# Sums of squares of the six pre-norms: TensorE reads the eight tiles of squares itself, VectorE adds nothing

## The reference

```
def _rmsnorm(x, w):
    xf = x.astype(jnp.float32)
    y = xf * lax.rsqrt(jnp.mean(xf * xf, -1, keepdims=True) + NORM_EPS) * w
    return y.astype(x.dtype)
...
    for i in range(DEPTH):
        hh = _rmsnorm(x, norm_w[i, 0])
        x = x + FFN_RES * _rmsnorm(_swiglu(hh, ...), norm_w[i, 1])
        hh = _rmsnorm(x, norm_w[i, 2])
        m = _even_mixer(hh, ...) if i % 2 == 0 else _odd_mixer(hh, ...)
        x = x + _rmsnorm(m, norm_w[i, 3])
        hh = _rmsnorm(x, norm_w[i, 4])
        x = x + FFN_RES * _rmsnorm(_swiglu(hh, ...), norm_w[i, 5])
```

## Time and profile before

| | |
|---|---|
| three runs | 3228.89, 3232.3, 3232.4 us; median 3232.3 |
| the profiled execution's own time | 3232.59 us |
| its span (first to last instruction) | 3230.8 us |
| mean granted TensorE clock | 0.933 |
| TensorE busy | 2871.7 us, 89% |
| DVE busy | 1560.4 us, 48% |
| ACT busy | 1034.4 us, 32% |
| DMA read | 240.79 MB, 75 GB/s |

### The profile page before, as it was taken

One profiled execution on the slowest core, in us unless ns is written; L12 is line 12 of the kernel. 1 busy time (PEld: TensorE's weight loads), 2 busy tenths in 40 slices (PEclk: granted clock), 3 DMA queues, 4 the chain that ended last, 5 costly groups with the idle time before them and its releaser, 6 DMA issues. The chain is left out here.

```text
span 3230.8 us, 37354 instructions
## 1 busy us (share of the span) xinstructions
PE 2871.7 (89%) x15512; PEld 2261.2 (70%) x15512; DVE 1560.4 (48%) x2191; ACT 1034.4 (32%) x1538; POOL 6.8 (0%) x10
## 2 busy tenths in 40 slices
PE   5999999999999997336779999999998769899998
PEld 1476677577888786226758888788886559778886
DVE  1157446635434533673256434553446476464244
ACT  0135334533223313330134223332233532342222
POOL 0000000000000000000000000000000000000000
PEclk9899979999999998667889999999998989999998
DMA  8121202112232332000012232233322110022322
GB/s 365 78 79 59 78 30 82 66 53 79 85 111 79 96 99 72 0 0 1 1 46 85 85 110 78 89 101 93 104 85 79 59 46 4 28 85 85 107 86 69
DMA packets 65112, 245.30 MB, mean 76 GB/s; under 512 B 7216, under 2 KB 7344, under 8 KB 63536
## 3 DMA queue, kind: packets, MB, share of 16 engines
q1 hardware_dynamic: 64656, 238.72, 22.8%
q0 software_dynamic: 288, 4.19, 0.4%
HBM read 240.79 MB, written 2.10 MB: 75 GB/s over the span
## 5 line engine op out<-in xcount | busy, mean ns | idle before, releaser
L346 PE MATMUL bank<-normed,weights_high 128*128 128x512 f32 x4848 | 1530.4, 397 | 45.8 <-ACT normed L1172 42.1
L346 PEld LDWEIGHTS bank<-normed,weights_high 128*128 128x128 f32 x4848 | 913.4, 190 | 272.9 <-issue 81.8
L346 PE MATMUL bank<-normed,weights_low 128*128 128x512 f32 x2424 | 953.1, 393 | 0.0
L1665 DVE TENSOR_TENSOR weights_low<-ring,weights_high 128x1024 fp32r<-128x1024 f32 (+2 forms) x431 | 484.5, 1127 | 516.8 <-ACT weights_high L1206 513.3
L1206 ACT ACTIVATE weights_high<-ring 128x1024 fp32r<-128x1024 f32 (+2 forms) x431 | 420.7, 979 | 934.6 <-PE bank L346 934.4
L346 PEld LDWEIGHTS bank<-normed,weights_low 128*128 128x128 f32 x2424 | 460.6, 190 | 96.9
L346 PE MATMUL bank<-hidden,weights_high 128*128 128x512 f32 x1408 | 433.3, 389 | 0.0
L346 PE MATMUL bank<-work 128*128 128x128 f32 (+7 forms) x1912 | 262.9, 354 | 74.5 <-DVE work L1936 50.2
L346 PEld LDWEIGHTS bank<-hidden,weights_high 128*128 128x128 f32 x1408 | 264.3, 188 | 54.8
L1880 DVE TENSOR_TENSOR silu_gate<-bank,rstd 128x512 f32<-128x512 f32 x176 | 120.9, 691 | 341.0 <-PE bank L346 336.1
L346 PE MATMUL bank<-hidden,weights_low 128*128 128x512 f32 x704 | 273.9, 389 | 0.0
(11 more groups left out here) (205 smaller groups left out, 1942.0 us busy)
## 6 DMA issues: line engine op xcount, KB each, us to landing
ring<-w_k SPq DMA_DIRECT2D x303, 512.0 KB, 3.5
work<-w_ada SPq DMA_DIRECT2D x6, 4096.0 KB, 20.9
ring<-w_d SPq DMA_DIRECT2D x64, 384.0 KB, 3.0
ring<-w_d SPq DMA_DIRECT2D x64, 320.0 KB, 2.9
work<-dft_in POOLq DMA_DIRECT2D x2, 2048.0 KB, 8.4
constants<-cst_in SPq DMA_DIRECT2D x1, 2656.0 KB, 8.9
residual<-x_in SPq DMA_DIRECT2D x1, 2048.0 KB, 13.6
out_dram<-residual SPq DMA_DIRECT2D x8, 256.0 KB, 2.1
```

Of the source, the lines that this page charges most:

```text
L346: return pe.matmul(o, lhsT, rhs, start=start, stop=stop, skip_group_check=True)
L1665: ve.tensor_tensor(WL[:, u % SPLIT, 0:w], RING[:, u % SLOTS, 0:w], WH[:, u % SPLIT, 0:w].bitcast(F32), ALU.subtract).then_inc(unit_split, 1)
```

## The change

`pre_rms` takes the place of the one-part call at all three places that a pre-norm's `rms_of` is called from: TensorE now reads all eight tiles of squares, waiting for ACT's `sq` of each, and adds them in bank 7. `sum_of_squares` is gone from VectorE's program.

```diff
@@ project, ffn, odd_projection (TensorE)
-                        rms_of(("pre", name), (tile(0), dve_done("sum", name)))
+                        pre_rms(name)
@@ TensorE
+            def pre_rms(name):
+
+                rms_of(("pre", name), *[(tile(k), act_done("sq", name, k)) for k in range(KT)])
@@ VectorE
-            def sum_of_squares(name):
-
-                for n in (4, 2, 1):
-                    for k in range(n):
-                        dve.wait_ge(*act_done("sq", name, k + n))
-                        if n < 4:
-                            dve.wait_ge(*dve_done("sums", name, 2 * n + k + n))
-                        d(ve.tensor_tensor(tile(k), tile(k), tile(k + n), ALU.add),
-                          *(("sum", name) if n == 1 else ("sums", name, n + k)), chain=False)
-
             def pre_norm(name, w, lows_first):
 
-                sum_of_squares(name)
                 for j in range(LEAD):
                     low(lows_first + j + SPLIT)
```

More of the change, by code:

```diff
@@ L658, in ffn @@
                         if q == 0 and j == LEAD:
-                            rms_of(("pre", f), (tile(0), dve_done("sum", f)))
+                            pre_rms(f)
                     u0, n = UNIT0[f"down{f}{q}"], half // 2
```

## The result

The changed kernel took 3305.7 us in the median of four runs (3301.8 to 3309.3), the kernel before 3232.35 in the median of its four beside it: a ratio of 1.0205, interval 1.0177 to 1.0233. The forecast was 3302. A second measurement, further down, gives 1.0204. Two single runs are left out of every ratio here, one of the kernel before at 4000.8 us and one of `two_tiles_mix0` at 3528.0, with mean granted clocks of 0.70 and 0.80.

A forecast was written before the change was run, and what follows sets the result against it. TensorE's stream was taken to set the time at the norms. Five norms at 12.5 us plus mix1 at 10.2 made 72.7 on 3232.3, or 3305.0, lowered to 3302; the 8-in-10 range was 3276 to 3317.

The forecast's parts named there:

- What bounds the kernel: At five norms TensorE's stream alone sets the time; behind mix1 it waits for chains of DVE and ACT.
- the two covers named for the additions: VectorE's 28.8 us of additions hide behind TensorE's first four units and DVE's 2.55 us idle before the reciprocal: 0 us.
- The passes: At each pre-norm, 56 added one-column passes at 0.112 us each cost 6.3 us at full clock.
- The clock: Falls to 0.50 about 2.9 us into each norm's passes: 3.9 us more on passes, 2.3 on work behind.
- the rival in which it holds: Clock stays 1.00 at the norms, so only the passes count: 37.6 us, 3270; chance 0.07 for all or most norms.
- the slow part behind: Low clock lasts 3.0 to 6.9 us behind each norm's passes and costs 1.4 to 3.2 us, taken as 2.3.
- Mix1: At this norm 6.3 + 3.9 lie before `ms`; TensorE's waits take up the 2.3 behind, so 10.2 us.
- The sum: Whole kernel: 5 x 12.5 + 10.2 = 72.7 us on 3232.3, giving 3305.0, lowered to 3302.
- Mixers hiding the delay: Rival: chains behind mix0 and mix1 have room for all their delay, leaving 50 us, 3282; chance 0.05.
- Nearly free passes: Rival: the 56 passes a norm take 0.025 us each, 8.4 us in all, without a clock fall: 3241; chance 0.02.
- Faster: Rival: additions were late for unit 4, so removing them saves at most 4.5 us a norm: 3213 at best; chance 0.01.

The follow-up runs named there:

- two_tiles_mix0: Kernel before, but at pre-norm mix0 alone VectorE does six of seven additions and TensorE reads two tiles, 8 passes more: ratio 0.9997.
- no_additions: Changed kernel, but TensorE reads tile 0 alone as before the change, and VectorE's 42 additions stay removed: 3236.5 us, ratio 0.9995.
- in_between: Changed kernel, but each tile's eight one-column passes stand behind that tile's three matmuls in the unit before: 3284.6 us, ratio 1.0143.
- half-width run: Changed kernel, but of tiles 1 to 7 only 64 of each 128 tokens are loaded as weights: 3277.7 us, ratio 1.0111.
- passes_alone: Kernel before with VectorE's 42 additions kept, but TensorE reads eight tiles behind the last addition: 3299.5 us, ratio 1.0191.

## Why the prediction was right, and where it was off

*What bounds the kernel* was read rightly. TensorE's stream sets the time at the norms, and `no_additions` gives back nothing, by its ratio and by its steps. Of the two covers named for the additions, TensorE's units were there. The idle 2.55 us before the reciprocal wasn't the second one: it stays as it was in `no_additions`, and what covered them on DVE is its wait for ACT's high part of unit 4.

*The passes.* 0.112 us at full clock and 6.3 us a norm: `in_between` shows 6.35 at five norms. The half-width run shows that the load makes the price.

*The clock.* It fell at all six, as in the layer norms, and the rival in which it holds fell with that. The size was off for the reason the prediction gave as open: behind dense products it holds longer, 3.9 to 5.0 us at five norms in place of 2.9. At pre-norm 10 the passes took 9.22 us where 26 at 0.112 and 38 at 0.214 make 11.0. So this term was 3.9 a norm and measured about 2.0; with the slow part behind, 6.2 was expected and 4.7 measured at the usual 10.2 us of half clock. The half clock lasted some 3 to 6 us behind the last pass, as forecast. A norm cost 11.1 where 12.5 was forecast (bounds 9.5 and 14.5; measured 9.4 to 12.7). The mean clock of the kernel was forecast at about 0.91 and was 0.921.

*Mix1* was forecast at 10.2, because the slow products behind `ms` would lie beside TensorE's waits. It cost 11.2. That step failed: the waits follow from the factor, and the factor needs `spread`, which stands behind twelve products of unit 4. DVE's timeline, one line of before (its reciprocal starts at 2474.45) and two of after:

```profile
2478.34 0.17 DVE L2064 TENSOR_SCALAR modulation<-vectors 128x14 f32<-128x14 f32 x1 [2.59 <-ACT rstd L1172]
...
2537.31 0.18 DVE L1659 RECIPROCAL rstd<-rstd 128x4 f32<-128x4 f32 x1 [10.56 <-ACT rstd L1176]
...
2544.23 0.17 DVE L2057 TENSOR_SCALAR modulation<-vectors 128x14 f32<-128x14 f32 x1 [5.61 <-ACT rstd L1176]
```

From the reciprocal to the first use of the factor it is 6.9 us, and was 3.9. The 3.0 us of twelve slow products and a slow spread are on that path. The number is near all the same, since the clock fell later than forecast: 8.0 us came ahead of the reciprocal, not 10.2.

*The sum.* 72.7 was worked out and 66.5 came at the norms. The median moved by 73.4, close to the forecast, because three of the first four runs of the kernel before were among its short ones: in 29 later runs it stands at 3243.9, and the difference to the changed kernel's second median is 63.8. A steady loss of about 66 us, 2.0%, is what the change does; the agreement to 4 us in the first result is partly luck.

*The rivals.* Mixers hiding the delay: mix0 lost 9.4 and 11.1 in two profiles of the changed kernel, mix1 11.2 and 11.1; nothing is hidden (the 9.4 has 6.8 us of half clock, and 01 lost as little with the same 6.8 in the second profile). Nearly free passes: they cost over four times the rival's 0.025 us. Faster: `no_additions` has nothing to gain.

## What to carry to other kernels

A sum over partitions by one-column matmuls costs what it loads as weights. With the constant ones as weights and the data moving, eight tiles cost about as much at full clock (6.6 us against 7.2), but the clock held and the spread fell away. Cheapest here is to let an engine with time to spare add first and hand TensorE one tile. On the engine that sets the time, look not only at how long added instructions take but at what they do to the clock of those behind: the eight passes that make a row of 16 cost only their own time, the 56 that make one of 64 cost three quarters of it once more. Before a difference of a few tenths of a per cent is explained, see whether an unchanged stretch of the kernel moves by as much from run to run.

## What the runs showed of the hardware that I had not expected

- TensorE's granted clock went from 1.00 to 0.50 while the profile has TensorE busy for 100% of the time: 2.3 to 5.0 us into rows of one-column passes behind dense products. With 32 passes (3.4 us) it fell at all six places, at five of them after the passes had ended, at the cost of the dense work behind them. With 16 it held at all six.
- The same 64 passes, eight at a time between three dense matmuls, left the clock at 1.00 at all six places.
- A float32 pass with one moving column took 0.112 us with 128 columns of weights and 0.059 with 64, at full clock.
- In a chain of small matmuls and VectorE work of 500 us, the time at half clock varied from 222 us (`passes_alone`) to 270 (`in_between`) with no change to its work, and its length from 498 to 519 us: 0.6% of the kernel, more than several of the edits tried here cost.
